# Two transformer blocks on one core: one padding tensor goes, another grows, and two tensors move down by 128 bytes

## The reference

```python
def reference(x, ...):
    x = first_block(x, ...)      # 2 layers
    return second_block(x, ...)  # 2 layers

# one layer of the first block
h = rmsnorm(x, norm_mix_pre[l]); proj = h @ w_in[l]      # 1024 -> 7168
# retention, a short and a 31-tap causal convolution, each followed by its own projection
merged = gates[:, :, 0] * y_ret + gates[:, :, 1] * y_sc + gates[:, :, 2] * y_cf
x = x + rmsnorm(merged @ w_o[l], norm_mix_post[l])
up = causal_dwconv(rmsnorm(x, norm_ffn_pre[l]) @ w_up[l], ffn_conv_w[l])
gate, val = jnp.split(up, 2, axis=-1)
x = x + rmsnorm((jax.nn.silu(gate) * val) @ w_down[l], norm_ffn_post[l])
# a layer of the second block: the same frame, with mLSTM, sparse and differential
# attention as its three branches, and silu(g) * u without a convolution
```

## The kernel before

| tensor | first byte | bytes | what it is |
|---|---|---|---|
| F | 1152 | 20480 | five pieces as loaded |
| H | 21632 | 20480 | their high parts |
| apart_low | 42112 | 128 | used by nothing |
| L | 42240 | 20480 | their low parts |
| X | 62720 | 8192 | the residual, 8 tiles of 256 |
| apart | 70912 | 64 | used by nothing |
| HH | 70976 | 8192 | high part of the activation |
| HL | 79168 | 8192 | low part of the activation |
| FH, FL | 87360, 101696 | 14336 each | the same for later products |
| POOL | 124736 | 83968 | 82 tiles of 256 |

## Time and profile before

### The profile page before, as it was taken

The page is one execution under the profiler, slowest core; times in us unless marked ns, Lnnn a source line. Parts: engine busy times, 40 slices in busy tenths (PEclk is TensorE's granted clock), DMA queues, the critical chain, the costliest instruction groups (busy, mean ns, idle before and its releaser), DMA issues.

```text
span 1839.2 us, 36333 instructions
## 1 busy us (share of the span) xinstructions
PE 1781.1 (97%) x14784; PEld 1734.7 (94%) x14784; DVE 1360.9 (74%) x2385; ACT 1072.6 (58%) x1808; POOL 190.8 (10%) x200
## 2 busy tenths in 40 slices
PE   8999999999999999999999999999999998999998
PEld 8999999999999989999999888999999988899998
DVE  6998789867899779876768867655557687676553
ACT  5455656654454657654775675544458757755442
POOL 1012410001002410001201003000002100030000
PEclk9999999999999999999999999999999999999999
DMA  8545536564645536664646634555555564355553
GB/s 284 178 151 186 191 122 202 194 206 134 204 161 184 184 127 206 195 205 140 192 147 170 202 103 141 177 198 194 194 156 180 160 195 132 106 169 194 196 194 104
DMA packets 90342, 320.08 MB, mean 174 GB/s; under 512 B 10528, under 2 KB 12992, under 8 KB 90048
## 3 DMA queue, kind: packets, MB, share of 16 engines
q1 hardware_dynamic: 90176, 317.75, 52.5%
HBM read 310.60 MB, written 1.08 MB: 169 GB/s over the span
## 4 chain that ended last, share of the span: by engine, by line
PE 73%; DVE 15%; ACT 6%; issue 4%; POOL 1%; DMA 1%; SPq 0%; DVEq 0%; ACTq 0%; POOLq 0%
PE big L588 67%; PE small L588 4%; DVE POOL L1467 4%; DVE L L1110 4%; ACT H L1886 2%; PE small L587 1%; DVE POOL L1299 1%; DVE POOL L1665 1%; ACT POOL L2270 1%; POOL POOL L2482 1%; ACT POOL L2308 1%; ACT L1982 0%; DVE gates L1354 0%; POOL POOL L2461 0%; DVE FL L1277 0%
## 5 line engine op out<-in xcount | busy, mean ns | idle before, releaser
L588 PE MATMUL big<-HH,H 128*128 128x256 f32 x3344 | 941.5, 282 | 9.6 <-DVE gates L1354 4.8
L588 PE MATMUL big<-HL,H 128*128 128x256 f32 x3344 | 927.4, 277 | 3.9 <-DVE HL L1245 3.8
L588 PE MATMUL big<-HH,L 128*128 128x256 f32 x3344 | 926.2, 277 | 0.0
L1110 DVE TENSOR_TENSOR L<-F,H 128x1024 fp32r<-128x1024 f32 x574 | 703.7, 1234 | 205.6 <-ACT H L1886 204.3
L1886 ACT ACTIVATE H<-F 128x1024 fp32r<-128x1024 f32 x582 | 610.7, 1055 | 205.7 <-PE big L588 202.2
L588 PEld LDWEIGHTS big<-HH,H 128*128 128x128 f32 x3344 | 630.1, 188 | 14.6 <-issue 5.9
L588 PEld LDWEIGHTS big<-HL,H 128*128 128x128 f32 x3344 | 630.3, 188 | 7.8 <-DVE HL L1245 5.9
L588 PEld LDWEIGHTS big<-HH,L 128*128 128x128 f32 x3344 | 629.9, 188 | 0.0
L588 PE MATMUL big<-FH,H 128*128 128x256 f32 x848 | 238.5, 281 | 0.0
L588 PE MATMUL big<-FH,L 128*128 128x256 f32 x848 | 234.4, 276 | 0.0
L588 PE MATMUL big<-FL,H 128*128 128x256 f32 x848 | 234.3, 276 | 0.0
(11 more groups left out here) (237 smaller groups left out, 1795.4 us busy)
## 6 DMA issues: line engine op xcount, KB each, us to landing
F<-in_stream SPq DMA_DIRECT2D x582, 512.0 KB, 4.1
POOL<-POOL SPq DMA_DIRECT2D x32, 128.0 KB, 4.0
POOL<-head_rows SPq DMA_DIRECT2D x8, 256.0 KB, 5.2
X<-in_x SPq DMA_DIRECT2D x2, 512.0 KB, 4.4
POOL<-POOL SPq DMA_DIRECT2D x16, 64.0 KB, 3.1
out_x<-X SPq DMA_DIRECT2D x1, 1024.0 KB, 3.9
POOL<-in_decay SPq DMA_DIRECT2D x1, 768.0 KB, 11.6
POOL<-POOL SPq DMA_DIRECT2D x8, 96.0 KB, 5.2
```

Source lines behind the costliest of these rows:

```text
L588: return pe.e.matmul(out_, lhsT, rhs, start=start, stop=stop)
L1110: v.tensor_tensor(L[:, j % NR, :], F[:, j % NF, :], H[:, j % NR, :].bitcast(F32), ALU.subtract).then_inc(s_lo, 1)
```

## The change

The padding tensor `apart_low` (32 float32, 128 bytes) between H and L is gone, and the padding `apart` between X and HH grows from 16 to 48 float32 (64 to 192 bytes). None of them is ever read or written. F, H, HH and everything behind HH stay where they are. L moves from byte 42240 to byte 42112, X from byte 62720 to byte 62592. No instruction, wait, loop or size is added, removed or reordered.

```diff
         F = sb("F", [P, NF, PB * P])
         H = sb("H", [P, NR, PB * P], F32R)
-        sb("apart_low", [P, 32])
         L = sb("L", [P, NR, PB * P], F32R)
         X = sb("X", [P, KT, T])
-        sb("apart", [P, 16])
+        sb("apart", [P, 48])
         HH = sb("HH", [P, KT, T], F32R)
         HL = sb("HL", [P, KT, T], F32R)
```

## The result

The changed kernel takes 1852.5 us (median of 9 runs, 1845.3 to 1868.6) against 1841.4 us for the kernel before in the same comparison (9 runs, 1838.2 to 1843.9). The ratio is 1.0065, with a 95% interval of 1.0037 to 1.0095: slower, by about 0.65%. It also scatters more, over 23 us instead of 6. Three further executions of the changed kernel are on record (1855.75 us, the profiled one, 1855.43 and 1843.69); with them it spans 1843.7 to 1868.6 us.

A forecast was written before the change was run, and what follows sets the result against it. TensorE, busy for 97% of the span, was taken as the bound. The terms, 0 + 0 + 0 + 0 on 1840.88 us, gave 1840.9 us, no change (0.72, 1835.4 to 1846.4); the 8-in-10 range was 1830 to 1852 us.

The forecast's parts named there:

- TensorE loading L: 4448 products loading L: L takes H's 192 bytes to the streamed tile, so 0 ns per load; bounds 30 us either way.
- Rival C: TensorE's products: L and H at the same phase disturb each other, 6.7 ns on 4448 products, 1871 us; chance 0.05.
- Rival A: TensorE's loads of L: the new place frees them of the 6.7 ns excess, 30 us faster, 1811 us; chance 0.09.
- Rival B: Line 1110: VectorE's write of L collides with its two reads, at the upper bound +31 us, 1872 us; chance 0.10.
- Rival D: Between long pieces: small duration changes shift the schedule 0.3 to 0.6% either way, 1830 to 1835 or 1846 to 1852 us; chance 0.04.
- VectorE, ScalarE, X and the DMAs: VectorE's writes of L, in-place instructions on X, X's first loads and the last store: all priced at zero.

The follow-up runs named there:

- l_alone: Kernel before with only L moved down 128 bytes, X kept at byte 62720: 1859.8 us, ratio 1.0094.
- three_h: Kernel before, layout unchanged, but TensorE loads H three times per block instead of H, H, L; VectorE still writes L: 1854.0 us, ratio 1.0092.
- all_up: Kernel before with 128 bytes of padding ahead of H, so H and all behind go up, distances between them kept: 1842.7 us, ratio 1.0003.
- l_up_256: Kernel before with 384 instead of 128 bytes in apart_low, so L and all behind go up 256 bytes: 1842.1 us, ratio 0.9993.
- narrow_0: H and L both at phase 0 (streamed tile's first byte less loaded block's, within 256), most products loading 64 of 128 weight columns: 1842.2 us.
- narrow: Kernel before, layout unchanged, all products except a group's first and last load 64 of 128 weight columns: 1835.9 us against 1842.6.
- swap_phase: Kernel before with 48 instead of 16 elements in apart, putting H at phase 64 and L at 192: 1861.0 us, ratio 1.0112.
- h0_l128: Kernel before with 32 instead of 16 elements in apart, putting H at phase 0 and L at 128: 1893.7 us, ratio 1.0287.
- both_128: Kernel before without apart_low and with 32 elements in apart, putting H and L both at phase 128: 1890.2 us, ratio 1.0272.

## Why the prediction was wrong

I forecast 1840.9 us and no change with 0.72; it is 1852.5 us, slower, just outside the range, and also beyond what I called within 0.3%.

**The step that failed** is "TensorE loading L": "With H and L on equal terms at two different phases, I price the move at 0 ns per load", because "the same thing, done with H at the new phase, costs the same". Its facts were right: H at 192 and L at 64 ran at the same rate, 113.3 ns. The inference was not, because the rate does not belong to one load at one phase: it depends on the phases of all three loads of a block together. Three loads at 192 can run fast or slow (the changed kernel, `l_alone`, `three_h`), at 113.5 or 117.9 ns per product; with 192 and 64 mixed as before, all four long pieces ran fast in each of the three profiled executions (before, `all_up`, `l_up_256`). So H's 113.3 ns were measured beside an L at 64, and did not hold beside an L at 192.

How that looks from within is seen at the start of the last long piece. Before, starts in us:

```profile
1654.22 0.35 PE L588 MATMUL big<-HH,H 128*128 128x256 f32 x1 [0.29 <-ACT HH L1919]
...
1654.81 0.28 PE L588 MATMUL big<-HH,L 128*128 128x256 f32 x1
1654.93 0.28 PE L588 MATMUL big<-HH,H 128*128 128x256 f32 x1
...
1655.87 0.28 PE L588 MATMUL big<-HH,L 128*128 128x256 f32 x1
1655.99 0.28 PE L588 MATMUL big<-HH,H 128*128 128x256 f32 x1
1656.10 0.28 PE L588 MATMUL big<-HL,H 128*128 128x256 f32 x1
1656.21 0.28 PE L588 MATMUL big<-HH,L 128*128 128x256 f32 x1
```

From 1654.81 to 1655.99 there are ten distances of 0.118 us on the mean: the burst of before starts at the slow rate too. Then the next products come after 0.11 us, and it stays so to the end. After:

```profile
1662.04 0.36 PE L587 MATMUL big<-HH,H 128*128 128x256 f32 x1 [0.29 <-ACT HH L1918]
...
1662.63 0.28 PE L587 MATMUL big<-HH,L 128*128 128x256 f32 x1
1662.75 0.28 PE L587 MATMUL big<-HH,H 128*128 128x256 f32 x1
...
1663.93 0.28 PE L587 MATMUL big<-HL,H 128*128 128x256 f32 x1
1664.05 0.28 PE L587 MATMUL big<-HH,L 128*128 128x256 f32 x1
1664.16 0.28 PE L587 MATMUL big<-HH,H 128*128 128x256 f32 x1
```

The thirteen distances from 1662.63 to 1664.16 are 0.118 us too, and so is the rest of the piece. Both enter it alike, after a wait of 0.29 us for HH. With L at 64 the slow spacing is left within a dozen products, with L at 192 it can last for 1583 of them. That the reads of a load meet the reads of the streamed tile at a certain offset in time, and that the spacing then settles, is my reading of this. Shown are the dependence on the distance (`all_up` and the table) and, at phase 0, on the loaded columns (`narrow_0`, with the reserve made there), not the cycle in which reads meet, nor what decides at a burst's start which rate it takes.

**Rival C**, "L and H at the same phase disturb TensorE", at a chance of 0.05, named the right engine, the right pair of tensors and the right sign. Its condition does not hold in general: unequal phases such as 192 / 128 (1.024) or 0 / 64 (1.021) are slower still. Its size was off in both ways: 6.7 ns on a third of the products everywhere gave +30 us; it is 4.4 ns (117.9 - 113.5) on all three products of a block, in some of the stretches, for most of 14.8 us of span and +11 us in the median. Its argument against ("two loads of one and the same block of H, at the same address") failed for the same reason as the step above.

**Rival A** is excluded. The 6.7 ns over the columns' own time stayed, or grew, at every pair of phases tried, and stayed in `narrow` with loads of half the length. What makes up those 6.7 ns is open. The 109.2 ns that the Trainium skill's figure for bare products (TensorE: Matmul & The Clock Gate, section "Wait — 56ns, not 53.3ns?") would give was reached in no run.

**Rival B** is excluded: line 1110 stayed at a median of 1218 ns with its write on its reads' phase, and `three_h` shows the slow rate without any change to it.

**Rival D**, a shift of the schedule between the long pieces, is there but small: the three steps with the clock add up to about 2 us in the profiled execution, and 7.0 of the 14.8 us arose inside a long piece. The prediction had taken the clock as "all at the higher level" from slices that are 46 us wide and show a 9 from 90% on; in that same execution it was 0.50 from 442.0 to 445.4 us.

**VectorE, ScalarE, X and the DMAs** were priced at zero, and that held: the medians of the instructions that write H, L and HL are within 1 ns, and `l_alone`, where X stays, is as slow as the changed kernel. The Trainium skill's rule on transfers that start off a 256-byte boundary (DMA: Bandwidth & Descriptors, section "How a descriptor splits into AXI transactions") cost nothing that could be told apart: X's loads land after 4.3 us (before 4.4) and the store after 4.0 (before 3.9, and an estimated 0.1 us by the rule).

**The range** took in D and lighter forms of A and B, and nothing of C, so that its upper end of 1852 us left no room for a slower rate of TensorE. With the bounds on TensorE's rate that the text itself had worked out, ±30 us, it would have held the result. I also wrote that I would be wrong if an interplay had "a period that is no divisor of 4096, or acts between two engines"; as far as tested it was neither (256 divides 4096, and `three_h` needs no second engine). An interplay of all three loads with the stream, with two lasting rates, was not on the list.

## What to carry to other kernels

When TensorE streams and loads without a pause, the distance in SBUF between the loaded block and the streamed tile can be a tuning parameter: here twelve pairs of phases lay between 1.000 and 1.035, with nothing else changed. Padding between tensors that looks idle may be holding such a distance, so check the spacing of products in every long burst before and after any change of the layout, also one that only resizes a tensor ahead. An argument from parts ("this address is fine for H, so it is fine for L") needs the case with all parts together, which one run of `three_h` would have given.

## What was not expected of the hardware

One sequence of instructions has two stable rates. In `l_alone` the same kind of piece took 175.49 us twice and, with more products, 179.69 and 179.71 us (117.9 and 113.5 ns per product) within one execution, at a granted clock of 1.00 in the windows inside a slow and a fast one. This would explain why the time of such a kernel scatters: the changed one ran from 1845.3 to 1868.6 us and `swap_phase` from 1849.2 to 1875.0, while layouts whose long pieces were all slow scattered less (`h0_l128`: 1893.5 to 1893.9 us, 4 runs; `both_128`, the widest, 1888.5 to 1894.6). No second trace of the same kernel was taken, so that the slow stretches move from one execution to the next is not shown directly.

The Trainium skill (SBUF — State Buffer, section "SBUF: two separate sides") says that TensorE's two read ports, one for the streamed operand and one for loads, are independent and that TensorE never waits on anyone. The runs do not bear out that loads and streams leave each other alone: the same loads and streams took from 113.5 to 120.2 ns per product by their distance alone, and at the worst distance loads of half the columns took the excess from 9.9 to 0.9 us. The measurement decides; whether the ports or something behind them is the place, no run shows. The rule holds between engines, as far as seen here: windows of before with VectorE busy for 112.22 and for 78.75 of 140 us hold the same 1238 products.
